# A two-layer hybrid decoder step: 30 groups of unused identity products where TensorE waits

## What is computed

```python
for l in range(2):
    h = rmsnorm(y, norm_mix_pre[l])
    m = mixer_ab(h) if l % 2 == 0 else mixer_cd(h)
    y = y + rmsnorm(m, norm_mix_post[l])
    y = y + rmsnorm(sq_relu_mlp(rmsnorm(y, norm_mlp_pre[l])), norm_mlp_post[l])
```

```python
v_new = u_c - w_c @ s
o = qg_c @ s + qk_c @ v_new
s = s * glast + kdec_c.T @ v_new
```

## Time and profile before

| | |
|---|---|
| median of three runs | 2959.62 us |
| the profiled execution | 2959.93 us |
| its span, first to last instruction | 2958.1 us |
| TensorE matmul (PE) busy | 2639.9 us, 89% |
| TensorE weight loads (PEld) busy | 2394.3 us, 81% |
| VectorE (DVE), ScalarE (ACT), GpSimd (POOL) busy | 42%, 32%, 30% |
| mean granted TensorE clock | 0.935 |

### The profile page before, as it was taken

One profiled execution on the slowest core, in us unless ns is written; L12 is line 12 of the kernel. 1 busy time (PEld: TensorE's weight loads), 2 busy tenths in 40 slices (PEclk: granted clock), 3 DMA queues, 4 the chain that ended last, 5 costly groups with the idle time before them and its releaser, 6 DMA issues. The chain is left out here.

```text
span 2958.1 us, 46930 instructions
## 1 busy us (share of the span) xinstructions
PE 2639.9 (89%) x19663; PEld 2394.3 (81%) x19663; DVE 1240.5 (42%) x2527; ACT 950.8 (32%) x1755; POOL 901.4 (30%) x453
## 2 busy tenths in 40 slices
PE   5878989998989999979978887989998888999998
PEld 5745878656889999978867787779996578999997
DVE  5754411576343222252655365541105453522224
ACT  3342231355342211152432343222214544311122
POOL 2241221133254333343343233313230004533331
PEclk9977999899999999989988898889999999999998
DMA  4202255451222222222201120112322262122221
GB/s 149 75 15 79 74 92 143 137 216 67 48 67 77 81 86 86 86 75 77 72 17 31 31 72 17 31 31 85 97 72 74 70 185 86 58 86 86 83 76 61
DMA packets 217568, 232.91 MB, mean 79 GB/s; under 512 B 40780, under 2 KB 186668, under 8 KB 216750
## 3 DMA queue, kind: packets, MB, share of 16 engines
q1 hardware_dynamic: 215278, 229.66, 25.5%
q10 hardware_dynamic: 2080, 0.25, 0.1%
HBM read 207.93 MB, written 48.35 MB: 87 GB/s over the span
## 5 line engine op out<-in xcount | busy, mean ns | idle before, releaser
L283 POOL TENSOR_TENSOR WRr<-WR,WH 128x2048 fp32r<-128x2048 f32 (+3 forms) x98 | 435.8, 4447 | 929.2 <-ACT WH L271 832.4
L2258 PE MATMUL PS<-HHr,WRr 128*128 128x288 f32 x1104 | 328.4, 297 | 0.0
L423 PE MATMUL PS<-HHr,WH 128*128 128x288 f32 (+1 forms) x928 | 282.8, 305 | 41.0 <-PEq L107 41.0
L423 PE MATMUL PS<-YTr,WRr 128*128 128x288 f32 x1024 | 304.0, 297 | 0.0
L271 ACT CAST WH<-WR 128x2048 fp32r<-128x2048 f32 (+3 forms) x98 | 180.3, 1840 | 335.8 <-DMA WR<-in_mlp_w 191.9
L423 PE MATMUL PS<-YTr,lt_WX 128*128 128x288 f32 x1408 | 281.8, 295 | 0.0
L423 PE MATMUL PS<-HTr,WH 128*128 128x288 f32 (+1 forms) x928 | 279.9, 302 | 0.0
L423 PE MATMUL PS<-HHr,WRr 128*128 128x288 f32 (+1 forms) x928 | 279.8, 302 | 0.0
L283 POOL TENSOR_TENSOR WRr<-WR,lt_WX 128x2048 fp32r<-128x2048 f32 x35 | 162.2, 4634 | 233.6 <-ACT lt_WX L271 233.6
L423 PE MATMUL PS<-WH,HHr 128*128 128x256 f32 (+3 forms) x760 | 219.5, 289 | 10.9 <-PEq L107 10.9
L423 PEld LDWEIGHTS PS<-YTr,lt_WX 128*128 128x128 f32 x1408 | 227.1, 188 | 0.1
(11 more groups left out here) (672 smaller groups left out, 6113.8 us busy)
## 6 DMA issues: line engine op xcount, KB each, us to landing
WR<-in_mlp_w SPq DMA_DIRECT2D x64, 1024.0 KB, 5.3
WR<-in_cd_w_in SPq DMA_DIRECT2D x34, 1024.0 KB, 5.4
out_dil_s<-in_cache_dil_kv SPq DMA_DIRECT2D x2, 7936.0 KB
WR<-in_ab_w_in SPq DMA_DIRECT2D x10, 1024.0 KB, 5.4
past_rows<-in_cache_nsa_kv SPq DMA_DIRECT2D x16, 256.0 KB, 3.4
WR<-in_ab_w_in SPq DMA_DIRECT2D x16, 256.0 KB, 4.3
WR<-in_nsa_ck_w SPq DMA_DIRECT2D x4, 1024.0 KB, 5.8
WR<-in_nsa_cv_w SPq DMA_DIRECT2D x4, 1024.0 KB, 5.4
```

The costliest lines, as they stand in the source:

```text
L283: pool.tensor_tensor(K.WRr[:, n % RING, 0:used], K.WR[:, n % RING, 0:used], high_slot(K, i, used).bitcast(F32), ALU.subtract).then_inc(K.l ...
L423: last = pe.matmul(out, a, b, start=(n == 0), stop=(n == 3 * len(terms) - 1))
L2258: last = pe.matmul(out, a[:, k, c], h[:, k, x], start=(n == 0), stop=(n == 3 * KT - 1))
```

## The change

A function `keep_busy(K, pe, out, n)` issues n plain products of the 128x128 identity with itself into a piece of PSUM that nobody reads. None of them signals a semaphore. It is called at these places of TensorE's order:

- at the end of layer 0's `project_conv`, behind a wait for the bank's last eviction: 22 products;
- at the end of `ssd_sample`: 18;
- in `layer_tail`: 16 (layer 0) or 26 (layer 1) ahead of the first L2156 of `A`, 14 behind L2150, 6 ahead of the second L2156; in layer 0, for `Z`, 32 ahead of the first L2156 and 12 behind L2150;
- in each `gdn_pair`: 12 behind the turns of L3150, 3 among the narrow products of the second head, 3 behind those of the first, 8 ahead of L3227, and 12 behind it, with two waits on ScalarE's counts.

Nothing is removed or reordered, and no other engine's instructions change. In all 30 calls issue 318 products.

```diff
--- before.py
+++ after.py
@@ -808,6 +808,9 @@
                     pe.matmul(K.PS[:, 6, :], K.ones[:], RS[:, i, 0:SEQ], start=True, stop=True)
                     pe.matmul(K.PS[:, 7, 0:TS], K.ones[:], RS[:, i, SEQ:TOK], start=True, stop=True).then_inc(summed, 1)
                 half_projection(K, pe, W, u % 2, u % pairs, 1).then_inc(K.mm, 1)
+            if not n_sums:
+                pe.wait_ge(raw_ready, 4 * (n_ch - pairs + 1))
+                keep_busy(K, pe, K.PS[:, 2 * (n_ch % pairs), 0:P], 22)
 
         def silu(act, u):
             act.wait_ge(conv_done, u + 1)
@@ -888,6 +891,13 @@
         sp.dma_start(out_p[0, :, at:at + n], rows[0:3, to:to + n]).then_inc(K.state_out, 16)
         sp.dma_start(out_s[:, :, at:at + n].rearrange("b s c -> (b s) c"), rows[3:27, to:to + n]).then_inc(K.state_out, 16)
     K.n_state_out += 2 * len(cols)
+
+
+def keep_busy(K, pe, out, n):
+
+
+    for _ in range(n):
+        pe.matmul(out, K.ident[:], K.ident[:], start=True, stop=True)
 
 
 def units_ahead(K, pe, W, halves):
@@ -1361,6 +1371,7 @@
                     yoff(b)
                     for i, j in place.get(2 * b + 1, ()):
                         update(i, j)
+                keep_busy(K, pe, turned_at(0)[:, 0:P], 18)
 
             @block.vector
             def _(dve):
@@ -2390,8 +2401,10 @@
                                 last.then_inc(K.mm, 1)
                             if b == 1 and o == 6 and c == 0:
                                 chain_ones1(K, pe, A, 0, 8)
+                keep_busy(K, pe, K.PS[:, 4, 0:P], (16, 26)[layer])
                 chain_ones2(K, pe, A, 0)
                 chain_ones1(K, pe, A, 1, 10)
+                keep_busy(K, pe, K.PS[:, 4, 0:P], 14)
                 first_pair(K, pe, [K.PS[:, j, 0:HALF] for j in range(2)], *split_wait(K, pe, up0), A)
                 for j, b in up_halves[2:]:
                     if b:
@@ -2400,6 +2413,7 @@
                     half_product(K, pe, K.PS[:, j, 0:HALF], wh, wl, slice((j % 2) * P, (j % 2 + 1) * P), b,
                                  A if j == 0 else None).then_inc(K.mm, 1)
                     if (j, b) == (2, 0):
+                        keep_busy(K, pe, K.PS[:, 4, 0:P], 6)
                         chain_ones2(K, pe, A, 1)
 
                 def up(r):
@@ -2444,9 +2458,11 @@
                     if (o, b) == (1, 1):
                         chain_ones1(K, pe, Z, 0, KT)
                 if layer == 0:
+                    keep_busy(K, pe, K.PS[:, 3, 0:P], 32)
                     chain_ones2(K, pe, Z, 0)
                     chain_ones1(K, pe, Z, 1, 2 * KT)
                     pe.wait_ge(acc_done, KT * LAST + 14)
+                    keep_busy(K, pe, K.PS[:, 3, 0:P], 12)
                     first_pair(K, pe, [K.PS[:, z_banks[i], 0:HALF] for i in range(2)], *split_wait(K, pe, gz), Z)
                     for i, (j, b) in enumerate(up_halves):
                         if i < 2:
@@ -3150,6 +3166,7 @@
                     last = pe.transpose(tile_(out, t), tile_(src, t), K.ident[:])
                 return last
 
+            spare, spare_1 = (K.PS[:, B[a].bank + 3, 384:384 + P] for a in range(2))
             for a, b in enumerate(B):
                 wide(a, b.A, K.ones[:], b.UG).then_inc(pes[a], 1)
                 wide(a, b.Bp, K.ones[:], b.IB).then_inc(pes[a], 1)
@@ -3164,6 +3181,8 @@
                 turn(b.A, b.k).then_inc(pes[a], 1)
                 pe.wait_ge(dves[a], DV["QKD"])
                 turn(b.Bp, b.v).then_inc(pes[a], 1)
+            pe.wait_ge(acts[0], AC["vb"])
+            keep_busy(K, pe, spare, 12)
             for a, b in enumerate(B):
                 pe.wait_ge(dves[a], DV["tok"])
                 turn(b.A, b.TT).then_inc(pes[a], 1)
@@ -3211,6 +3230,10 @@
                     c = slice(r * NS, (r + 1) * NS)
                     pe.matmul(out[:, :, c], b.S0[:, r, :], b.big[:, 4:6, SEQ + r * NS:SEQ + (r + 1) * NS],
                               start=(r == 0), stop=False, skip_group_check=True)
+                    if a and r == NB // 2:
+                        keep_busy(K, pe, K.PS[:, 0, 0:P], 3)
+                if a == 0:
+                    keep_busy(K, pe, K.PS[:, 0, 0:P], 3)
                 pe.matmul(out[:, 1, :], b.vb[0:TS, SEQ:TP], b.TT[0:TS, SEQ:TOK], start=False, stop=True,
                           skip_group_check=True).then_inc(pes[a], 1)
             for a, b in enumerate(B):
@@ -3221,12 +3244,15 @@
                 pe.wait_ge(acts[a], AC["VN4"])
                 pe.matmul(K.PS[:, b.bank + 3, 256:256 + TS], b.VN4, b.QKD[0:TS, SEQ:TOK], start=False, stop=True,
                           skip_group_check=True).then_inc(pes[a], 1)
+            keep_busy(K, pe, K.PS[:, 0, 0:P], 8)
             for a, b in enumerate(B):
                 pe.wait_ge(dves[a], DV["VNm"])
                 for half in range(2):
                     last = pe.matmul(K.PS[:, b.bank + half, :], b.kdec[0:TS, SEQ:TP], b.VNm[:, 4 * half:4 * half + 4, :],
                                      start=True, stop=True)
                 last.then_inc(pes[a], 1)
+            pe.wait_ge(acts[1], AC["O"])
+            keep_busy(K, pe, spare_1, 12)
 
 
 
```

## The result

The changed kernel takes 2966.5 us (median of 7 runs, 2964.9 to 2974.4) where the kernel before takes 2959.9 (7 runs, 2958.9 to 2961.6): a ratio of 1.0025 with a 95% interval of 1.0015 to 1.0034. It is slower by 6.6 us; the forecast was 18.5 us faster. The profiled execution took 2967.3 us, 7.4 more than that of the kernel before.

What follows compares the result with a forecast made beforehand. TensorE, busy 89% of the span, was taken as the bound, with its time at 1.2 GHz the target. Terms -1.5 - 1.5 - 1.0 - 7.3 - 8.7 + 1.5 = -18.5 us took 2959.9 to 2941.4; 8-in-10 range 2932 to 2954.

Steps and rivals of the forecast that it cites:

- the one on the ends of the pairs: Ends of the four pairs: added products cost +0.4 us a pair, +1.5 in all; bounds -0.9 and +7.7 a pair.
- the ends give back what the heads gain: Clock falls in each narrow stretch, back by the last 12 products: +2.0 us a pair, 2947.8 us; chance 0.12.
- the slower rival: Clock falls at each pair's end and does not recover there: +7.7 us a pair, 2979 us; chance 0.06.
- The middles: Middle of the pairs: 12 products in the 4.01 us wait for VectorE keep the clock up behind it: -7.3 us.
- the first rival: Turns do not hold the clock in the pairs' middles, so the 7.3 us go: 2948.7 us; chance 0.10.
- The heads of pairs 2 and 4: Eight wide products at the start of pairs 2 and 4 run at full clock: -2.7 and -1.5 us.
- the products behind pair 2: Norm stage behind pair 2: 25 products that ran at 0.50 run at full clock: -2.7 us.
- the third rival: Middles and heads do not wait for TensorE's speed; half of 7.3 + 8.7 is lost: 2955.9 us; chance 0.09.
- The end of the projection stage: Layer 0: 22 products fit the 5.46 us wait, and the 14 records behind run at full clock: -1.5 us.
- the sample's state updates: End of that stage: 18 products fit 5.07 us idle, and the next stage's 14 records run faster: -1.5 us.
- The end norm: End norm: ScalarE waits for the second of two sums, which would be shorter at 2.4 GHz: -1.0 us.
- the middle norm: Middle norms: taken as 0 because ScalarE loads a table there; bounds a loss of 1 and a gain of 3.

Runs made afterwards that it cites:

- run with 3 products more: Changed kernel with 32 one-column products, 3 more products in the first head's narrow ones and 9 in place of the last 12: 2947.4 us, ratio 0.9965.
- the pair of runs above: Changed kernel with 32 one-column products and without all five norm groups, 2961.7 us; and the changed kernel itself run once more, 2966.9 us.

## Why the prediction was wrong

**The step that failed is the one on the ends of the pairs.** It priced two outcomes rightly: +0.4 us a pair if the clock holds, up to +7.7 if it falls and does not recover. The run with 3 products more has the first (+0.2 a pair against the kernel before), pair 3 of the changed kernel nearly the second (+6.6). But it chose between the two by "I am near the lower end", from a count of 14 dense products, although the row beside it showed the clock falling while TensorE was listed as busy throughout. The four ends cost 2.4, 4.8, 6.6 and 3.2 us. The price follows the low time: in the changed kernel an end takes 15.4 us and half of each low microsecond (15.4 + 3.4, 15.4 + 5.1, 15.4 + 8.5). The ends of the kernel before follow the same line with 10.4 for 15.4, to 0.3 us. By these two lines the 26 products cost 5 us an end and break even there only if they save 10 us of low clock, nearly all that there is (9.8 to 14.2 us). The line does not reach down to no low time: with as many products and none of it, the ends of the run with 3 products more take 16.1 and 16.8 us. So with 26 products there was at best nothing to win within an end, and what a held clock earns it earns behind it.

**The rival "the ends give back what the heads gain" had the mechanism** (the clock falls in each narrow stretch and is back by the last 12) in three pairs of four, with +2.0 us a pair where it was +3.5; in pair 3 it was the slower rival's. The two should not have had 0.12 and 0.06 beside 0.63 for the forecast: a count of fillers is no evidence that a stretch will hold.

**Right, term by term.** The middles came out at -7.3 us, to a tenth, at 1.00 in all four pairs. The 20 turns ahead of the filled wait did not let the clock fall, so the first rival is out. The Trainium skill (TensorE: Matmul & The Clock Gate, Part 4: PE-mode transpose) says that the full clock does not engage for transposes, and the rows do not bear it out: turns ran at 1.00 behind 4.7 us of turns alone, and no middle had a low stretch. The heads of pairs 2 and 4 gained 2.6 and 1.4 us (forecast 2.7 and 1.5), the products behind pair 2 the 2.7 that they should. TensorE's speed was what the middles and heads waited for, which leaves the third rival out. The end of the projection stage gained 1.5 us and that of the sample's state updates 1.3 (forecast 1.5 and 1.5), alike in all ten profiled executions that have these groups; the changed kernel's was 1.0 us ahead already when it reached the first of them. The end norm gained 1.0 in the pair of runs above (1.0) before it was given back, and the middle norm nothing, as written.

**A gain early in the program did not reach pair 1.** The 4 us had gone by the time pair 1 began (+0.9), and the same holds in the ten profiled executions that have both early groups: pair 1 begins between 1491.1 and 1497.0, on average at 1494.7, against 1494.0 in the four without. In the changed kernel's own profiled execution the gain went in clock: three stretches of unchanged work have more of it low. 30.0 us at 0.93 became 33.2 at 0.84 (from 494 us on), 17.0 at 0.98 became 19.5 at 0.78 (from 731), and 15.0 at 0.77 became 17.3 at 0.70 (from 1389). The prediction allowed 5 us either way for such chance, without a sign. In seven of the other nine a collision comes on top. In the changed kernel run again, the timelines of VectorE and GpSimd read:

```profile
724.36 4.93 DVE L2112 TENSOR_SCALAR q_E<-q_E,q_sm,a_GS 128x264 f32<-128x264 f32 x2
...
724.29 4.51 POOL L283 TENSOR_TENSOR WRr<-WR,WH 128x2048 fp32r<-128x2048 f32 x1 [15.03 <-ACT WH L271]
```

and in the kernel before:

```profile
725.01 0.74 DVE L2101 TENSOR_SCALAR q_E<-q_E,q_sm,a_GS 128x264 f32<-128x264 f32 x2
...
725.53 4.60 POOL L283 TENSOR_TENSOR WRr<-WR,WH 128x2048 fp32r<-128x2048 f32 x1 [12.40 <-ACT WH L271]
```

Two small VectorE operations take 0.74 us when GpSimd's weight piece starts behind them, and 4.93 when it starts 0.07 us ahead; TensorE then waits 4.8 us for them instead of 1.7. The Trainium skill (SBUF — State Buffer, Who interferes with whom) calls the port pair of VectorE and GpSimd an exclusive lock that the first comer holds for a whole instruction; these rows agree. At 700 us the seven are 2.8 to 9.7 us ahead of the kernel before; the three without the collision are 2.7 us ahead at most. From 712 to 735 us the seven lose 6.5 us each, and the three lose nothing. About half of the 6.5 goes before the collision, in low stretches that the kernel before does not have there (0.79 for 1.00), and half from it on. No run took either away by itself, so which brings the other is not shown.

**What no step had: the stall for instructions, 6.6 us.** The prediction counted each added product by its time on TensorE and not by its place in the stream. The Trainium skill (Runtime: NRT & Kernel Launch, Instruction fetch mechanics) has instructions refilled in 16 KiB blocks and calls the crossing mostly hidden. In this stage, whose DMA engines are busy 0.7 to 0.8 of the time, it is hidden at most places and not at one: moving the stream by 64 places made the stage 6 us longer, by 128 no longer, and the same 128 on top of the change took 6 us off. The packets of 16384 bytes agree with the size. That late pieces are the cause is shown twice over: the loss goes with the place in the stream, and every longer standstill in this stage ends just behind the landing of a piece. How the 6.6 us come of 7.4 us of standing (1.8 before) is less plain: by the windows most of it is work at the lower clock, 21 us of it instead of 11, and that the clock fell because TensorE stood is argued, not shown.

So of the 26 us between the forecast and the profiled execution, 15.5 are the ends, 6.7 the stall and 4.9 the early gains that did not arrive, less 1.8 that came behind the pairs beyond the forecast; the rest is under 1. Without the stall no difference from the kernel before can be told (1.0005, 0.9995 to 1.0014).

## What to carry to other kernels

Fillers that lay in a wait cost nothing, and in the middles their gain was forecast to a tenth; fillers on the path paid only where the clock held all through, so price both outcomes, and build the group until the windows read 1.00 in every copy of the stretch: here three products in another place, in a kernel rid of its stall, made 13 us. In this case the clock fell although the engine was busy, in thin products, and counting the fillers did not tell whether they would suffice. A gain early in a long program need not reach its end; compare start times along the whole of it. When an edit to a long instruction stream gives a loss far from where it was made, look for "issue" waits in a stage that keeps the DMA engines busy, compare their ends with the packets of the instruction queue, and move the stream by some harmless instructions before judging the edit.

## What the runs showed of the hardware

- The granted clock fell while TensorE was listed as busy, with less than 0.1 us idle since the end began, 3.1 to 5.8 us into the narrow products of 16 columns and the small products behind them (all four ends of the kernel before). It stayed at 2.4 GHz with 9 identity products among the narrow ones and 8 behind them (four of four ends of one profiled execution); with 6 and 8 it held in two ends of four in one kernel and in none of four in the changed kernel.
- TensorE stood still for up to 3.0 us in a row of small products, with nothing to wait for that the profile shows, in a stage with its DMA engines busy 0.7 to 0.8 of the time. Whether it did hung on the place of the code in its instruction stream (72 or 79 us for the same stage, in one profiled execution of each kernel; the times of the kernels with and without it lie 6 to 8 us apart over 7 to 12 runs each). The 38 standstills of 0.4 us or more all ended 1.2 to 1.7 us behind the end of a 16384-byte packet of the instruction queue.
- Two VectorE operations on SBUF took 4.93 us instead of 0.74 when a GpSimd operation of 4.5 us began 0.07 us ahead of them. In the kernel before, where the GpSimd operation began 0.5 us behind their start, they were not held, but a copy of 128x4 that came 3.4 us into it took 1.25 us instead of 0.17, until the GpSimd operation ended.
